# Splitting the shift columns off three modulation sums, and reordering the third mixer's work between copies, maxima, accumulation jobs and low parts

## The reference

```python
shift, scale, gate = split(c @ mod_w + mod_b, 3)          # one modulation per half, six in all
h = rms_norm(x, w_in) * (1 + scale) + shift
y = mixer(h)   or   swiglu(h)   or   conv_glu_ffn(h)
x = x + gate * rms_norm(y, w_out)                         # blocks one and two
x = x + gate * y                                          # block three (adaLN), then a final rmsnorm
```

## Time and profile before

| | |
|---|---|
| median of 3 runs | 1062.88 us (1061.72 to 1063.24) |
| the profiled execution | 1063.47 us, of which the span of the trace is 1061.7 us |
| PE, PEld busy | 94%, 91% of the span |
| DVE, ACT busy | 75%, 53% |
| mean granted clock of PE | 0.979 of full speed |
| transfers | 227.59 MB, mean 214 GB/s |

### The profile page before, as it was taken

The page is one execution under the profiler, slowest core; times in us unless marked ns, Lnnn a source line. Parts: engine busy times, 40 slices in busy tenths (PEclk is TensorE's granted clock), DMA queues, the critical chain, the costliest instruction groups (busy, mean ns, idle before and its releaser), DMA issues. The chain is left out here.

```text
span 1061.7 us, 21373 instructions
## 1 busy us (share of the span) xinstructions
PE 1003.0 (94%) x8136; PEld 968.5 (91%) x8136; DVE 794.0 (75%) x1316; ACT 559.9 (53%) x1126; POOL 4.6 (0%) x14
## 2 busy tenths in 40 slices
PE   6999889999999999989999999999997989999996
PEld 5998678899999999979999999998886989999995
DVE  4756885798888777877778888876867558877775
ACT  2444674544444455554454444445654466677663
POOL 0100000000000000000000000000000000000000
PEclk9998998999999999999999999999998999999998
DMA  9967667288878755831648888774613234554541
GB/s 362 335 200 217 237 220 261 79 332 301 298 301 307 267 214 198 302 116 33 226 173 303 297 299 303 289 265 159 252 59 99 81 100 166 191 178 180 186 147 42
DMA packets 62409, 227.59 MB, mean 214 GB/s; under 512 B 7010, under 2 KB 7266, under 8 KB 61956
## 3 DMA queue, kind: packets, MB, share of 16 engines
q1 hardware_dynamic: 61556, 224.02, 58.9%
q0 software_dynamic: 640, 2.10, 0.8%
q10 hardware_dynamic: 144, 0.52, 0.1%
HBM read 225.04 MB, written 1.57 MB: 213 GB/s over the span
## 5 line engine op out<-in xcount | busy, mean ns | idle before, releaser
L1957 PE MATMUL bank<-hH,wH 128*128 128x258 f32 (+1 forms) x1544 | 444.2, 288 | 12.4 <-DVE hL L1328 9.4
L1958 PE MATMUL bank<-hL,wH 128*128 128x258 f32 (+1 forms) x1544 | 438.0, 284 | 0.0
L1959 PE MATMUL bank<-hH,wL 128*128 128x258 f32 (+1 forms) x1544 | 436.4, 283 | 0.0
L1263 DVE TENSOR_TENSOR wL<-raw,wH 128x1024 fp32r<-128x1024 f32 x270 | 328.0, 1220 | 48.3 <-ACT wH L804 47.1
L1957 PEld LDWEIGHTS bank<-hH,wH 128*128 128x128 f32 x1544 | 292.4, 189 | 20.5 <-issue 13.4
L804 ACT ACTIVATE wH<-raw 128x1024 fp32r<-128x1024 f32 x270 | 276.5, 1047 | 42.2 <-PE bank L1959 23.6
L1959 PEld LDWEIGHTS bank<-hH,wL 128*128 128x128 f32 x1544 | 293.7, 190 | 0.0
L1958 PEld LDWEIGHTS bank<-hL,wH 128*128 128x128 f32 x1544 | 293.2, 190 | 0.4
L1957 PE MATMUL bank<-aH,wH 128*128 128x256 f32 x592 | 170.4, 288 | 3.0 <-DVE wL L1263 3.0
L1959 PE MATMUL bank<-aH,wL 128*128 128x256 f32 x592 | 169.6, 287 | 0.0
L1958 PE MATMUL bank<-aL,wH 128*128 128x256 f32 x592 | 169.6, 287 | 0.0
(11 more groups left out here) (337 smaller groups left out, 1157.9 us busy)
## 6 DMA issues: line engine op xcount, KB each, us to landing
raw<-in_weights SPq DMA_DIRECT2D x270, 512.0 KB, 4.6
modbuf<-in_mod_w SPq DMA_DIRECT2D x69, 512.0 KB, 6.0
modbuf<-in_w_ada SPq DMA_DIRECT2D x36, 512.0 KB, 6.7
strips<-in_mod_w SPq DMA_DIRECT2D x16, 512.0 KB, 6.8
strips<-in_w_ada SPq DMA_DIRECT2D x12, 512.0 KB, 7.1
strips<-bias_table POOLq DMA_DIRECT2D x8, 256.0 KB, 6.4
otok<-in_cmp_w SPq DMA_DIRECT2D x4, 512.0 KB, 9.1
raw<-in_mod_w SPq DMA_DIRECT2D x2, 512.0 KB, 4.3
```

The lines of the kernel that those rows point to most:

```text
L1263: V.tensor_tensor(wL[:, slot, :], raw[:, slot, :], wH[:, slot, :].bitcast(F32), ALU.subtract).then_inc(lo_ready[c], 1)
L1957: mm(out, lhs_h, rhs_h, start=start, stop=False, skip_group_check=True)
L1958: mm(out, lhs_h, rhs_l, start=False, stop=False, skip_group_check=True)
L1959: return mm(out, lhs_l, rhs_h, start=False, stop=stop, skip_group_check=True)
```

## The change

In the three seams whose shift and scale were summed together, the scale columns stay ahead of the last unit of y and the eight shift columns become a sum of their own (`modS1`, `modS2`, `modS4`, in banks 1, 5 and 5), put after the gate columns; `keep_clock` behind them is cut from six to three matmuls. `first_pair` now waits for the shift to be taken. In `norm_b` (DVE) the order of `scaled`, the takes and `raw_low` changes, in `raw_a` (ACT) `shift_high` goes behind the first `raw_high`; both also hold for seam 3. In `sb`, DVE's `copy_first(2)` and `pair_max(3)` go ahead of the low parts and jobs, ACT's `exp_pair(2)`, `copy_second(2)` ahead of its high parts, and the eight columns of `modG4` go behind `token_out(3)`, in bank 7.

```diff
-        MOD_COLUMNS = {"modA1": ((1, 0, 16),), "modG0": ((0, 16, 24),), "modA2": ((2, 0, 16),), "modG1": ((1, 16, 24),),
-                       "modA3": ((3, 8, 16), (2, 16, 24)), "modS3": ((3, 0, 8),), "modA4": ((4, 0, 16),),
...
+        MOD_COLUMNS = {"modA1": ((1, 8, 16),), "modG0": ((0, 16, 24),), "modS1": ((1, 0, 8),),
+                       "modA2": ((2, 8, 16),), "modG1": ((1, 16, 24),), "modS2": ((2, 0, 8),),
+                       "modA3": ((3, 8, 16), (2, 16, 24)), "modS3": ((3, 0, 8),), "modA4": ((4, 8, 16),),
+                       "modG3": ((3, 16, 24),), "modS4": ((4, 0, 8),), "modA5": ((5, 0, 16),), "modG5": ((5, 16, 24),),
...
-            return bank[{"modA1": 6, "modG5": 4, "modG4": 5}.get(name, 7)]
+            return bank[{"modA1": 6, "modS1": 1, "modS2": 5, "modS4": 5, "modG5": 4}.get(name, 7)]
...
@@ ACT, raw_a
-                shift_high(a)
+                act.wait_ge(sc_ready, a)
                 act.wait_ge(sq_used, 4 * n)
                 for b in range(4):
                     raw_high(a, 2 * b)
+                    if b == 0:
+                        shift_high(a)
                     raw_high(a, 2 * b + 1)
                     raw_square(a, b)
@@ ACT, sb
-            split_upto(base + 18)
             exp_pair(2)
+            copy_second(2)
+            split_upto(base + 17)
+            exp_pair(3)
+            split_upto(base + 18)
-            split_upto(base + 20)
-            copy_second(2)
-            exp_pair(3)
             copy_second(3)
@@ DVE, norm_b
                 scaled(0)
-                scaled(1)
-                mod_take(late)
+                if late != SHIFT_OF[a]:
+                    mod_take(late)
+                else:
+                    scaled(1)
+                    mod_take(late)
                 for b in range(4):
...
                     if b == 0:
+                        if late != SHIFT_OF[a]:
+                            scaled(1)
+                            mod_take(SHIFT_OF[a])
                         shift_low(a)
-                    if b < 2:
-                        scaled(b + 2)
+                    if b == 1:
+                        scaled(3)
                     raw_low(a, 2 * b)
                     raw_low(a, 2 * b + 1)
+                    if b == 0:
+                        scaled(2)
@@ DVE, sb
             pair_max(2)
-            split_upto(base + 18)
-            jobs_upto(JOBS_END["sb"])
             copy_first(2)
             pair_max(3)
             mod_take("modG5")
-            split_upto(base + 20)
+            split_upto(base + 17)
             copy_first(3)
             dve.wait_ge(prob_ready, 40)
             row_factor(32, None)
+            split_upto(base + 18)
             dve.wait_ge(pv_done, 40)
...
-            mod_take("modG4")
+            jobs_upto(JOBS_END["sb"] - 2)
             dve.wait_ge(an_in, 1)
...
+            jobs_upto(JOBS_END["sb"])
             split_upto(base + 22)
...
             mix_low(2)
             mix_low(3)
+            mod_take("modG4")
             shift_low(5)
@@ PE
             norm_sums("B0")
             mod_sum("modG0")
-            keep_clock(bank[1], 6)
+            mod_sum("modS1")
+            keep_clock(bank[0], 3)
...
             pair_pv(2)
-            mod_sum("modG4")
             pair_turn(3)
...
                 token_out(i, base + 14 + i)
+            mod_sum("modG4")
             for b in range(4):
                 attention_out(b, base + 18 + b)
```

More of the change, by code:

```diff
@@ L367, in build_program @@
         MISC = ["table", "mod0s", "mod0h", "bc", "gates", "gatesT", "cmpk", "cmpv", "vrep", "cscore",
-                "modA1", "modG0", "modA2", "modG1", "modA3", "modS3", "modA4", "modG3", "modA5", "modG5", "modG4"]
-        MOD_COLUMNS = {"modA1": ((1, 0, 16),), "modG0": ((0, 16, 24),), "modA2": ((2, 0, 16),), "modG1": ((1, 16, 24),),
-                       "modA3": ((3, 8, 16), (2, 16, 24)), "modS3": ((3, 0, 8),), "modA4": ((4, 0, 16),),
-                       "modG3": ((3, 16, 24),), "modA5": ((5, 0, 16),), "modG5": ((5, 16, 24),),
+                "modA1", "modG0", "modS1", "modA2", "modG1", "modS2", "modA3", "modS3", "modA4", "modG3", "modS4",
+                "modA5", "modG5", "modG4"]
+        MOD_COLUMNS = {"modA1": ((1, 8, 16),), "modG0": ((0, 16, 24),), "modS1": ((1, 0, 8),),
[3 rows of a table added]
                        "modG4": ((4, 16, 24),)}
-        SHIFT_OF = {1: "modA1", 2: "modA2", 3: "modS3", 4: "modA4", 5: "modA5"}
+        SHIFT_OF = {1: "modS1", 2: "modS2", 3: "modS3", 4: "modS4", 5: "modA5"}
         def mod_bank(name):
-            return bank[{"modA1": 6, "modG5": 4, "modG4": 5}.get(name, 7)]
+            return bank[{"modA1": 6, "modS1": 1, "modS2": 5, "modS4": 5, "modG5": 4}.get(name, 7)]
         misc = {name: i for i, name in enumerate(MISC)}
@@ L533, in cd_jobs @@
             return JOBS_END["f0"] + min(2 * e // 3 if e < 18 else e - 7, 2 * KT)
-        JOBS_FOR = {"modA1": JOBS_END["modA1"], "modG0": JOBS_END["ab"], "modA2": JOBS_END["f0"] - KT,
+        JOBS_FOR = {"modA1": JOBS_END["modA1"], "modG0": JOBS_END["ab"], "modS1": JOBS_END["modA1"],
+                    "modA2": JOBS_END["f0"] - KT, "modS2": JOBS_END["f0"] - KT, "modS4": JOBS_END["f1"] - KT,
                     "modG1": JOBS_END["f0"], "modA3": JOBS_END["cd"], "modS3": JOBS_END["cd"],
@@ L845, in shift_high @@
                                      ACT.Copy).then_inc(sh_ready, 1)
-                act.wait_ge(sc_ready, a)
             def raw_high(a, k):
@@ L1206, in _ @@
             qk_rs(4)
+            exp_pair(2)
+            copy_second(2)
+            split_upto(base + 17)
+            exp_pair(3)
             split_upto(base + 18)
-            exp_pair(2)
+            copy_second(3)
             split_upto(base + 20)
-            copy_second(2)
-            exp_pair(3)
-            copy_second(3)
             act.wait_ge(otok_ready, 2)
@@ L1224, in _ @@
             shift_high(5)
+            act.wait_ge(sc_ready, 5)
             act.wait_ge(sq_used, 4 * NORMS.index("A5"))
@@ L1984, in mod_sum @@
             def mod_sum(name):
-                if name not in ("modG5", "modG4"):
+                if name not in ("modG5", "modG4", "modS1", "modS2", "modS4"):
                     misc_free(name)
@@ L2029, in first_pair @@
                     sum_square(n, 3)
-            FIRST_AFTER = {1: "modG0", 2: "modG1", 3: "modS3", 4: "modG3", 5: "modG4"}
+            FIRST_AFTER = {1: "modS1", 2: "modS2", 3: "modS3", 4: "modS4", 5: "modG4"}
             def turn_values(phase, e):
@@ L2439, in _ @@
             mod_sum("modG1")
-            keep_clock(bank[5], 6)
+            mod_sum("modS2")
+            keep_clock(bank[4], 3)
             def stick_z(h):
@@ L2517, in _ @@
             mod_sum("modG3")
-            keep_clock(bank[5], 6)
+            mod_sum("modS4")
+            keep_clock(bank[4], 3)
             def qk_sums(n):
@@ L2647, in _ @@
                     pe.wait_ge(an_out, 2)
-                    pe.wait_ge(misc_taken, misc["modG4"] + 1)
+                    pe.wait_ge(misc_taken, misc["modG5"] + 1)
                     for b in range(2):
```

## The result

The changed kernel took 1056.12 us (median of 6 runs, 1051.07 to 1058.5) against 1063.06 us (6 runs, 1061.41 to 1065.84) for the kernel before: ratio 0.9927, 95% interval 0.9899 to 0.9956. It is faster by 6.9 us where 11.1 was forecast, and the time lies above the range of 1049.8 to 1054.8. The profiled execution took 1056.86 us with a span of 1055.1 us (1063.47 and 1061.7 before).

What follows compares the result with a forecast made beforehand. PE's work plus its idle and slow stretches bounds the kernel. Seams 1, 2, 4 give 3.3 us, seam 3 -0.4, the third mixer 8.15, say 11.1: from 1063.47 to 1052.4 profiled, 1051.8 as median; range 1049.8 to 1054.8.

Steps and rivals of the forecast that it cites:

- seam 3: At seam 3, `raw_low(2)` and PE's third tile come 0.4 us later: -0.4 us, bounds 0 and -0.65.
- the clock stays at 1.00 from 815 to 822: Third mixer: PE's clock at 1.00 where it ran at 0.50 from 813 to 822; a sign the forecast (0.5) is right.
- rival 1: Third mixer: the clock falls around pair 3, costing 1.65 us, partly hidden; gain 9.5 to 10.3, 1052.6 to 1053.4; chance 0.27.
- The rule of the Trainium skill: Frequent short idle stretches between matmul groups swing PE's clock; here one fall worse, up to 1053.4.
- seams 1, 2, 4, each: PE starts 1.65 us sooner, but its third-tile wait grows from 0.41 to about 1.1: gain 1.05 to 1.15 each.
- (a): Third mixer: the 5.86 us wait and slow clock go, `token_out(0)` at 815.7 against 825.87: 10.2 us gained.
- (b): Third mixer: DVE's queued work behind `token_out(0)` moves the first residual to P + 18.4 from P + 16.35: -2.05 us.
- (c): From the residual to `f2`'s fifth tile, 13.2 us later, the gain carries on; the 1.71 us wait remains, at 1.5.
- Rival 2: The seams give nothing, a new wait replacing the old: gain 7.8 us, 1055.1; chance 0.08.
- P: Start of `token_out(0)` in the third mixer, from which the tail is counted; forecast at 815.7 against 825.87.
- rival 3: Mixer's tail worse: DVE's 15 us chain behind P waits for high parts or transfers; with 2 us, 1053.8; chance 0.11.
- The other side: Slower than before: long clock falls at all three seams cost 15.1 us and give 1067; chance 0.02.

Runs made afterwards that it cites:

- before_filled: The kernel before with 22 unused matmuls in the 5.86 us wait ahead of `pair_pv(2)`: 1060.75 us, ratio to before 0.9971.
- seams_only: The kernel before with only the seams' edits, the third mixer's order as before: 1062.35 us, ratio to before 0.9974.
- seam_order: The changed kernel with `scaled(2)` moved ahead of `shift_low` in all four seams: 1057.03 us, ratio to before 0.9938.
- fill_last: The changed kernel with four unused matmuls ahead of `pair_pv(3)` alone: 1055.49 us, ratio to before 0.9901.
- after_filled: The changed kernel with 12 unused matmuls in PE's four short waits of the third mixer: 1054.26 us, ratio to before 0.9902.
- after: The changed kernel itself, first comparison and profile: 1056.12 us, ratio to before 0.9927.
- all_orders: The changed kernel with fillers, `scaled(2)` ahead of `shift_low`, and one low and one high part behind pair 3's copies: 1050.96 us, ratio to before 0.9903.
- all_orders_b: all_orders repeated unchanged on a third chip: 1053.06 us, ratio to before 0.9891.
- after_b: The changed kernel repeated unchanged on a third chip: 1053.98 us, ratio to before 0.9906.

## Why the prediction missed, point by point

**The step that failed** is "the clock stays at 1.00 from 815 to 822", the forecast's own condition, to which it gave 0.5 against 0.27 for rival 1. Rival 1 is what happened: a fall around pair 3 in five profiles of five. The argument against it was that each idle piece is shorter than any that was followed by a fall. Each piece is (0.35, 0.44, 1.09 us, 1.9 us idle within 3.2), and the fall came all the same. The fillers show that these waits bring it about. The rule of the Trainium skill that the prediction set against itself ("TensorE: Matmul & The Clock Gate", section on depth-cycling in PSUM) had this sign, and the traces around pair 3 agree with it: 5 falls in 5 unfilled profiles, 0 in 6 filled ones. Its price was rival 1's too, 1.65 at most; measured 1.0 and 2.6.

The sum of the short waits doesn't tell either. At seam 1 of the kernel before, PE is idle 1.57 and 0.41 us within 3.7, as much as around pair 3, and the clock stays at 1.00:

```profile
188.00:192.00 4.00, 2.43 (x22) 2.27 (x21) 3.93 (x12) 1.43 (x3) 0.00 (x0) 1.00 0.07 30
192.00:196.00 4.00, 3.59 (x27) 3.29 (x26) 3.82 (x11) 2.86 (x6) 0.00 (x0) 1.00 0.00 0
```

At seam 3 of the changed order it is idle 1.30 and 1.00 us within 4.0, and no fall follows in any profile. Nor is one wait always answered alike: the 1.79 us of the earlier trace rows are followed by a fall within 2 us in ten of the thirteen profiles that have them. So why this place has a fall each time and the seams have none stays open.

"The clock falls not in the wait but behind it" is wrong for the longest wait. In the kernel before it falls ahead of 813 us, about 2 us before the 5.86 us wait ends at 814.77; between 812 and 813 PE does nothing and the mean clock is 0.85:

```profile
812.00:813.00 1.00, 0.00 (x0) 0.00 (x0) 0.90 (x2) 0.00 (x0) 0.00 (x0) 0.85 0.44 176
```

**The sum without the clock was nearly right.** The mean granted clock of each run gives how long it ran at half rate: (1 - clock) x 2 x span. For the changed kernel that is 37.6 us on average over 18 runs, for the one before 43.0 (46 runs). A run's time less half of that is 1036.3 against 1042.7, a gain of 6.4 us. The forecast without its 4.1 us of clock is 6.95. The other 2.7 us of the 9.1 are the clock: 5.4 us fewer at half rate, where 8.2 were forecast. This split is rough, since time at half rate inside a wait costs nothing: by the same reckoning *before_filled*, which has only fillers in a wait beside the kernel before, comes to 1044.9, 2.2 us above it.

| term | forecast | in the traces |
|---|---|---|
| seams 1, 2, 4, each | 1.05 to 1.15 | 1.0 |
| seam 3 | -0.4 | -0.5 |
| (a) to `token_out(0)`, no fall | 10.2 | 10.03 |
| (b) given back to the first residual, no fall | -2.05 | -1.47 |
| (c) carried on to `f2` | 0 | 0 |
| the fall around pair 3 | 0 | -1.0 or -2.6 |

The changed kernel's three profiles had falls of 2.6, 1.0 and 1.0, 1.5 on average: 3.0 - 0.5 + 10.03 - 1.47 - 1.5 = 9.6, against the 9.1 of the runs, whose standard error is some 0.6. Without a fall the terms make 11.1, the forecast to a tenth, and that is in part luck: the seams and (a) came out 0.6 lower in all, (b) 0.6 higher.

**Seams.** The trade was as worked out: PE's first wait shrinks, the second grows from 0.41 to 0.99 since `scaled(2)` moved behind `raw_low(1)`. Only the split was off: 0.64 and 0.99 where 0.4 and 1.1 were forecast. The gain per seam is 1.79 + 8.79 - 9.57 = 1.0 us (8.79 is 193.45 less the start of the sums of squares of before, 184.66). Rival 2 (they give nothing) falls: *seams_only* has the distances and a ratio below one. *seam_order* confirms the cause of the second wait, since it goes back to 0.41 there.

**The mixer's tail.** `attention_out(0)` at P + 15.6 instead of 14.85 looks like rival 3, but is the clock's doing: without a fall it is P + 14.35 and the residual P + 17.81. DVE's chain was costed 0.6 too long. *fill_last* shows that nothing waits there otherwise: its distances are *after_filled*'s. Rival 3 falls.

**The other side** was out of reach: at the seams the clock stands at 1.00 in every profile, and the lowest clock of a run of the changed kernel was 0.978.

**The level and the range.** The change's own miss is 11.1 - 9.1 = 2.0 us, and the fall costs 1.0 to 2.6. The rest of the distance from 1051.8 to 1056.12, 2.3 us, is level and scatter, 1.1 in the kernel before and 1.2 in the six runs of the changed one. The three runs of the kernel before on which the forecast stood had a median 1.1 us below that of 52 runs, and falls elsewhere vary from one execution to the next: the 0.50 stretch in the second mixer around 460 us lasts 3.4 us in one profile and 17.1 in another. The changed kernel's 18 runs follow it: the eight with a mean clock of 0.985 or 0.986 took 1051.07 to 1053.72 us, the ten of 0.978 to 0.981 took 1054.38 to 1058.5. The range left no room for this.

**What stays open.** A second fall, at 799.8 to 806.6 us in *after*, follows the 1.30 us wait ahead of `pair_scores(2)`, and costs 3.3 us. It is there in two of nine profiles in which that wait is not filled (*after* and *seam_order*) and in none of five with the filler. PE's order and that wait are the same before the change, so the edit is not its cause as far as the order shows; but both falls are among the six profiles with the new order of the mixer, none among the three with the old one, and such counts don't tell chance from cause. Nor do the runs show why the fall around pair 3 lasts 3.4 us in three profiles and 6.8 in two; both of the long ones also have the fall at 800 us.

**A version that beats both?** *all_orders* and its repeat have 12 runs with a median of 1052.38 us (1048.0 to 1057.51) and a mean of 1052.2 (standard error 0.7), against 1055.1 (0.5) for the changed kernel: 2.9 us less, or 11.9 below the mean of before, 1064.1. The traces account for 1.6 at the seams and, to the residual, 1.4 or 3.0 around pair 3 (26.88 or 28.47 less 25.49). The fillers alone have a mean of 1054.1 (12 runs, 0.6), 0.9 below the changed kernel, which is inside the error of both; their effect is shown in the trace, not in the time. These means pool runs from different chips. On the one chip that timed both, *all_orders_b* is 0.9 us under *after_b* by the medians and 1.7 by the means.

## What to carry to other kernels

When a change takes a long wait off TensorE, don't count the clock as given back because each wait that is left is short. Neither the length of one wait nor the sum of several told here where the clock would fall. Price a fall (here 1.0 to 2.6 us) and try a few unused matmuls in the waits that are left: here they took only time that TensorE waited anyway, and no profile that had them shows the fall. When an operation is moved ahead of a latency, ask what it used to hide: `scaled(2)` was free under ACT's latency and cost 0.35 us per seam once it stood behind it. And for differences of a few microseconds in a kernel of 1 ms, compare distances between marks on either side of the edit and the mean granted clock of each run, beside the medians: six runs of one kernel moved their median by 2 us.

## What was not expected of the hardware

- A fall of the clock to 0.50 at the end of or behind 1.9 us of idle time in three pieces, none over 1.09 us, in five profiles of five, while 1.98 us in two pieces at a seam was followed by none. With eight matmul records in the last of the three pieces it stayed at 1.00, in the one profile that had them alone.
- The length of the low stretches around pair 3 was 3.4, 6.8 or 10.2 us in the seven profiles that have one: 3.4 or 6.8 with the three short waits, 10.2 with the wait of 5.86 us, within which it begins.
- The changed kernel ran at half rate for some 29 to 46 us per execution, partly in places that differ from one execution to the next; half of that difference is 8.5 us, and its 18 runs cover 7.4.
